# Routed rows of a top-2 expert layer: scattered once into a table sorted by turn and fetched by plain loads, in place of an indirect gather per turn

## The reference, cut to what matters

```python
g_prob = softmax(t @ w_grp + b_grp);  g_idx = top_k(g_logits, 1)          # 1 of 4 groups
e_in_group = (t @ w_exp + b_exp)[group of the token]
top_v, top_i = top_k(e_in_group, 2);  top_w = softmax(top_v) * g_w        # 2 of 4 experts
a = einsum('td,edf->tef', t, w_gate_e);  u = einsum('td,edf->tef', t, w_up_e)
hid = silu(a) * u * combine[..., None]
return einsum('tef,efd->td', hid, w_down_e)                                # D_EXPERT = 512
```

## Time and profile before

| | |
|---|---|
| time, median of 3 executions | 1935.51 us (1934.56 to 1939.46) |
| span of the profiled execution | 1934.0 us |
| PE / DVE / ACT / POOL busy | 91% / 28% / 11% / 8% of the span |
| DMA over the span | 531.09 MB, 275 GB/s |
| software (POOL) queue | 97.15 MB, 14.1% of 16 engines |
| chain that ended last, PE / issue / DMA / DVE | 65% / 12% / 10% / 5% |

### The profile page before, as it was taken

How to read it: one execution, slowest core, us unless ns; L and a number is a source line. 1 busy time by engine, 2 the same in 40 slices (tenths; PEclk the granted TensorE clock), 3 DMA queues, 4 the chain that set the end, 5 groups by cost and what they waited for, 6 DMA issues and landing times.

```text
span 1934.0 us, 27785 instructions
## 1 busy us (share of the span) xinstructions
PE 1767.3 (91%) x11144; PEld 1114.0 (58%) x11144; DVE 534.1 (28%) x1152; ACT 210.8 (11%) x405; POOL 156.1 (8%) x274
## 2 busy tenths in 40 slices
PE   7799999999998999978889999997699998998998
PEld 4366666666666877756667777775333333333335
DVE  3100000000047744455553111003323222231233
ACT  2010000000001201102222100002110001000002
POOL 1011111111110001410000000000100000000000
PEclk9899999999999999988899999998799899999999
DMA  9997887677516335538999874242499999999992
GB/s 371 402 380 273 317 297 285 246 262 289 198 49 201 100 111 168 207 119 298 385 392 368 325 271 134 88 174 94 146 368 406 397 397 384 410 404 383 401 391 96
DMA packets 154570, 531.09 MB, mean 275 GB/s; under 512 B 17701, under 2 KB 61899, under 8 KB 131803
## 3 DMA queue, kind: packets, MB, share of 16 engines
q1 hardware_dynamic: 128834, 432.24, 58.9%
q0 software_dynamic: 17088, 97.15, 14.1%
q10 hardware_dynamic: 8578, 0.73, 0.4%
HBM read 510.94 MB, written 19.15 MB: 274 GB/s over the span
## 4 chain that ended last, share of the span: by engine, by line
PE 65%; issue 12%; DMA 10%; DVE 5%; SPq 4%; DVEq 1%; POOL 1%; ACT 1%; POOLq 1%; ACTq 0%; PEldq 0%
PE ps L652 62%; DMA ring<-in_w_up_e_dram 4%; DMA ring<-in_w_ada_dram 2%; PE ps L662 2%; SPq L399 2%; DMA xT<-in_w_ada_dram 2%; SPq L393 2%; DMA xT<-in_w_in_dram 2%; POOL work L537 1%; DVE z L1468 1%; DVE z L1459 1%; DVEq L2115 1%; DVE ring L1465 1%; POOLq L536 0%; DVE ring L1837 0%
## 5 line engine op out<-in xcount | busy, mean ns | idle before, releaser
L652 PE MATMUL ps<-hT,ring 128*128 128x288 f32 x2304 | 585.3, 410 | 5.3 <-PE ps L652 3.6
L652 PEld LDWEIGHTS ps<-hT,ring 128*128 128x128 f32 x2304 | 430.0, 190 | 169.7 <-issue 59.1
L652 PE MATMUL ps<-ring,work 128*64 128x512 f32 (+1 forms) x1280 | 273.4, 617 | 25.3 <-DMA ring<-in_w_ada_dram 12.2
L652 PE MATMUL ps<-z,ring 128*128 128x288 f32 (+1 forms) x1040 | 255.5, 407 | 4.5 <-PE ps L652 2.7
L1468 DVE COPY z<-ps 128x256 f32<-128x256 f32 (+7 forms) x98 | 64.3, 660 | 677.1 <-PE ps L652 656.9
L652 PE MATMUL ps<-ring,z 32*32 32x256 f32 (+3 forms) x3744 | 213.9, 396 | 21.2 <-DVE z L1468 11.2
L652 PEld LDWEIGHTS ps<-z,ring 128*128 128x128 f32 x1040 | 196.4, 190 | 62.8 <-issue 7.5
L652 PEld LDWEIGHTS ps<-ring,work 128*64 128x64 f32 (+1 forms) x1280 | 77.8, 134 | 181.4 <-issue 165.7
L652 PEld LDWEIGHTS ps<-ring,z 32*32 32x32 f32 (+3 forms) x3744 | 108.5, 114 | 115.2 <-issue 108.3
L1263 ACT ACTIVATE z<-ps 128x512 f32<-128x512 f32 (+4 forms) x108 | 60.1, 602 | 860.3 <-PE ps L652 850.4
L1465 DVE SCALAR_TENSOR_TENSOR xT<-ps,modT,xT 128x256 f32<-128x256 f32 x160 | 70.8, 480 | 254.3 <-PE ps L652 254.2
(11 more groups left out here) (209 smaller groups left out, 877.4 us busy)
## 6 DMA issues: line engine op xcount, KB each, us to landing
ring<-in_w_in_dram SPq DMA_DIRECT2D x36, 2048.0 KB, 14.3
ring<-in_w_gate_e_dram SPq DMA_DIRECT2D x32, 2048.0 KB, 12.7
ring<-in_w_up_e_dram SPq DMA_DIRECT2D x32, 2048.0 KB, 18.4
ring<-in_w_down_e_dram SPq DMA_DIRECT2D x32, 2048.0 KB, 15.0
ring<-in_w_ada_dram SPq DMA_DIRECT2D x16, 2048.0 KB, 20.5
z<-in_w_ada_dram POOLq DMA_DIRECT2D x32, 1024.0 KB, 7.9
xT<-in_w_ada_dram POOLq DMA_DIRECT2D x32, 1024.0 KB, 6.7
ring<-in_cache_v_dram SPq DMA_DIRECT2D x64, 512.0 KB, 5.8
```

Source lines behind the costliest of these rows:

```text
L652: return nc.tensor.matmul(o, lhsT, rhs, start=start, stop=stop, skip_group_check=free)
```

## The change

The table `h_rows` goes; in its place stands `h_sorted`, with NWIN * W = 1664 rows of 8 KB, row `at_turn * 64 + at_slot`. At `ob_ready`, behind the load of `x_kept`, POOL zeroes 4 KB in each partition of `work2` and writes it over the whole table with 13 DMAs of 1 MB. DVE computes the six columns of destinations (`places`) and signals `places_ready` before the rest of the list; POOL then issues six indirect DMAs, each scattering 96 rows of `hTok` (each token twice). DVE waits for the clears before it writes `listing`, and for the scatters before it clears `y_two`. SP fetches the 64 rows of turn 0 after the scatters, those of turn 1 after `hs_turned` 1, and in the loop those of turn w + 2 between the fourth and the fifth weight load of turn w + 1. POOL's loop is gone.

```diff
@@ SP
+            def sorted_rows(turn):
+                sp.dma_start(hg, h_sorted[ds(turn * W, W), :]).then_inc(sem("hg_full"), 16)
-            def expert(e, turn):
+            def expert(e, turn, rows_of=None):
                 for n in range(6):
                     s = (MOE + n) % SLOTS
+                    if n == 4 and rows_of is not None:
+                        sp.wait_ge(sem("hs_turned"), rows_of)
+                        sorted_rows(rows_of)
                     sp.wait_ge(sem(f"ring_free{s}"), turn + freed(MOE + n))
...
             expert(0, 0)
+            sp.wait_ge(sem("rows_sorted"), 16 * 2 * NT)
+            sorted_rows(0)
+            sp.wait_ge(sem("hs_turned"), 1)
+            sorted_rows(1)
             sp.wait_ge(*step("table_ready"))
...
-                expert(e, w + 1)
+                expert(e, w + 1, w + 2)
@@ POOL
             pool.dma_start(xflat, x_kept).then_inc(sem("x_back"), 16)
+            pool.memset(cleared, 0.0)
+            pool.drain()
+            for n in range(NWIN * W // P):
+                pool.dma_start(h_sorted[n * P:(n + 1) * P, :].rearrange("p (a n) -> p a n", a=2),
+                               cleared.unsqueeze(1).to_broadcast([P, 2, 1024])).then_inc(sem("rows_cleared"), 16)
...
-            for c in range(NT):
-                pool.wait_ge(sem("htok_copied"), 4 * c + 4)
-                pool.dma_start(h_rows[c * TT:(c + 1) * TT, :], hTok[:, c, :]).then_inc(sem("h_stored"), 16)
-            def gather(w):
-                pool.tensor_copy(take, token_i[:, ds(w, 1)])
-                pool.drain()
-                pool.indirect_dma_start(hg, None, h_rows, bass.IndirectOffsetOnAxis(ap=take, axis=0)).then_inc(sem("hg_full"), 16)
-            pool.wait_ge(sem("h_stored"), 16 * NT)
-            pool.wait_ge(*step("list_ready"))
-            gather(0)
-            pool.wait_ge(sem("hs_turned"), 1)
-            gather(1)
+            pool.wait_ge(*step("places_ready"))
+            pool.wait_ge(sem("htok_copied"), 4 * NT)
+            pool.wait_ge(sem("rows_cleared"), 16 * (NWIN * W // P))
+            for i in range(2 * NT):
+                pool.indirect_dma_start(h_sorted, bass.IndirectOffsetOnAxis(ap=places[:, i:i + 1], axis=0),
+                                        hTok[:, i // 2, :], None).then_inc(sem("rows_sorted"), 16)
...
-            with pool.Fori(0, last_turn) as it:
-                pool.wait_ge(sem("hs_turned"), it + 2)
-                gather(it + 2)
@@ DVE
             pick(at_slot, within)
+            pick(at_turn, turn)
+            stt(places, at_turn, float(W), at_slot, ALU.mult, ALU.add)
+            v.drain()
+            v.sem_inc(reach("places_ready"), 1)
             tt(in_slot, ...)
-            pick(at_turn, turn)
...
+            v.wait_ge(sem("rows_cleared"), 16 * (NWIN * W // P))
             for n in range(2):
                 tt(listing[:, :, :, n], ...)
...
-            copy(token_i, sums[0:W, :, 0])
             copy(listed, sums)
-            v.drain()
-            v.sem_inc(reach("list_ready"), 1)
             nc.vector.memset(spots, 0.0)
-            v.wait_ge(sem("h_stored"), 16 * NT)
+            v.wait_ge(sem("rows_sorted"), 16 * 2 * NT)
             nc.vector.memset(y_two, 0.0)
```

More of the change, by code:

```diff
@@ L63 @@
         "gla_sample_ready os_turned_copied ms_a_ready rs_a_ready rs_a_inverted "
-        "kv_tok_ready gla_scratch_free f_ready s_new_copied ob_ready work_free ms2_ready logits_copied member_ready pos_ready "
-        "table_ready list_ready").split(),
+        "kv_tok_ready gla_scratch_free f_ready s_new_copied ob_ready work_free ms2_ready logits_copied member_ready places_ready pos_ready "
+        "table_ready").split(),
 }
@@ L125, in build @@
         eps_col = vcol[:, 150:151]
-        h_rows = nc.dram_tensor("h_rows", [T, D], F32).ap()
+        h_sorted = nc.dram_tensor("h_sorted", [NWIN * W, D], F32).ap()
         x_kept = nc.dram_tensor("x_kept", [P, KT * T], F32).ap()
@@ L248, in build @@
         now = ms[:, 2 * NWIN:2 * NWIN + 2]
-        token_i = rstd[0:W, 0:NWIN].bitcast(I32)
-        take = rstd[0:W, 64:65].bitcast(I32)
+        places = rstd[0:TT, 0:2 * NT].bitcast(I32)
+        cleared = work2[:, 0:1024]
         spots = z[:, 3 * D:3 * D + T]
@@ L639, in _ @@
                                vcol[:, V_GF:V_GF + KT].unsqueeze(2).to_broadcast([P, KT, P]), ALU.mult).then_inc(sem("gf_spread"), 1)
-            last_turn = pool.value_load(wtab[0:1, 1:2], min_val=NE - 1, max_val=NWIN - 3)
-            with pool.Fori(0, last_turn) as it:
-                pool.wait_ge(sem("hs_turned"), it + 2)
-                gather(it + 2)
             pool.wait_ge(sem("gla_prompt_stored"), 16)
```

## The result

| | before | after |
|---|---|---|
| median | 1935.65 us (1934.56 to 1939.46, 4 runs) | 1967.89 us (1961.33 to 1972.5, 4 runs) |
| span of the profiled execution | 1934.0 us | 1959.8 us |
| router's logits product to the first product of turn 0 | 40.3 us | 52.7 us |
| first product of turn 0 to the end of the span | 556.5 us | 568.5 us |

The changed kernel is slower: ratio 1.0159, 95% interval 1.0133 to 1.0185, 32.2 us on the medians. That is under 2%, but clear of the noise. The prediction was no change, 1935.0 us, with a range up to 1949.

A forecast was written before the change was run, and what follows sets the result against it. The prediction took DMA to bound the turns, with PE close behind. The loop's -10.5 us and the start's +10 us gave -0.5 us, all other terms 0: 1935.0 us on the median, no change, range 1925 to 1949.

The forecast's parts named there:

- What bounds the kernel: In the turns: DMA engines fully busy at 395 GB/s, slowed behind each gather, with PE close behind.
- PE's cap: In the turns: 18 us is all PE can give back, from weight waits and the lower clock after them.
- The loop, -10.5 us: Plain loads replacing 15 gathers lose 1.7 us each instead of 2.4, saving 0.7 us a turn.
- The place in the queue, 0: In the loop: the fetch standing behind the gate and up loads on SP's queue costs nothing.
- The cover: In the loop: 32 PE products, 7.8 us, hide the fetch; without them it costs up to 2.5 us a turn.
- Rival 1: In the loop: the destination causes the dip, so the loop gives 0 and the start costs 10 us: 1945.5 us; chance 0.27.
- The rule on the ports: For fetches onto partitions 0 to 63: only 8 of 16 DMA ports are reached, so transfers run at half rate.
- Rival 2: In the loop: only the gather is slow, plain rows cost their bytes, PE becomes the bound: 1927.5 us; chance 0.18.
- Rival 3: Before the turns: scatters slower than stores (start +15) or clears reaching PE: 1942 us, 1950 with rival 1; chance 0.10.
- The start, +10 us: Before the first turn: six serial scatters, then SP's load, delay the first product by 10 us, ends 5.5 and 15.
- The clears, 0: Writing 13.6 MB during the PE-bound up projections hides in idle DMA capacity; at most a few us otherwise.
- The clear of `y_two`, 0: Before the first turn, behind the scatters: its 2 us hide under the fetch and the transposes, 8 us.

The follow-up runs named there:

- r3_actq: Changed kernel, with ACT issuing the loop's plain fetches on its own DMA queue instead of SP: 1945.55 us, ratio 1.0065.
- r9_poolq: Changed kernel, with POOL issuing every fetch of sorted rows as a plain DMA on its software queue: 1946.7 us, ratio 1.0051.
- r2_wide: Changed kernel, with each loop fetch writing the same 512 KB onto 128 partitions of 4 KB (rows partly wrong): 1932.2 us, ratio 0.9987.
- r5_shift: Changed kernel, with each loop fetch writing its 64 rows onto partitions 32 to 95 instead of 0 to 63 (wrong rows): 1933.61 us, ratio 0.9992.
- r8_pair_gather: Kernel before, with one indirect gather of 128 rows onto 128 partitions for every two turns, full computation: 1922.0 us, ratio 0.994.
- r7_clears: Kernel before, with only the 13 clears added, to a table nobody reads, and DVE waiting for them before the list: 1934.63 us, ratio 0.9999.
- r6_half_bytes: Changed kernel, with each loop fetch cut to 4 KB of each of the 64 rows, same partitions (wrong rows): 1932.1 us, ratio 0.999.

## Why the prediction was wrong, point by point

- **What bounds the kernel: right.** The turns are bound by DMA, the loss sits in the dips, and PE stands close behind. PE's cap was put at 18 us; the kernels without dips have a rest of 540 to 544 us where before has 556.6, so it is 12 to 17 us.
- **The loop, -10.5 us: the first step that failed.** It took the plain fetch to lose 1.7 us instead of the gather's 2.4, from the one plain narrow load in the trace of before, scaled by bytes. Measured in the turns, the plain fetch's dip loses 2.3 to 2.4 us from a second queue, the gather's 2.5, and the rests are 556.2 and 557.3 us against 556.6: the saving is 0. The load of 32 rows was a poor sample. It ran in another stage among other loads, and a dip of 2 us between stretches that are themselves unsteady gives a loss with little precision.
- **The place in the queue, 0: the second and larger one.** It cost +18.4 us (rest 575.0 against 556.6). The cover held, PE never waits for the rows. But the step looked only at who waits for the fetch. That the fetch in the weights' own queue would slow the weights more than it did in a second queue wasn't asked. r3_actq and r9_poolq against after show it.
- Together the two steps make 10.5 + 18.4 = 28.9 us of the miss of 32.9. The ends that were put on a fetch's loss, 0 to 2.4 us, held no value above the gather's, although nothing in the trace ruled one out. The range therefore had no room for a loop that gets worse.
- **Rival 1, that the dip belongs to the destination: right in its mechanism** (r2_wide, r5_shift, r8_pair_gather), and r3_actq and r9_poolq are that rival as it was priced, 1945.5 us against 1945.55 and 1946.7. That the first agrees to 0.1 us is luck: its start cost 12.3 us and not 10, and its router began 2.1 us earlier. Its evidence was in rows 10 and in the lone gather of rows 8; it was given 0.27 where the forecast had 0.45. The change as built adds the queue's 18 us to it. The rule on the ports that spoke against the change (the Trainium skill, "SBUF — State Buffer", section "Door 1: The DMA port swizzle") thus held in direction. The estimate of a 1.2 us loss from its 218 GB/s is under all that was measured in the turns for a whole fetch onto these partitions, 2.3 to 3.1 us in the dip.
- **Rival 2, that only the gather is slow: wrong.** A plain load dips as deep or deeper. **Rival 3, slower scatters or clears that reach PE: wrong** as priced: the start stayed under its +15 us and the clears cost nothing.
- **The start, +10 us: right**, 12.4. The terms: from the places to the last row in the table 18.5 us predicted, from the first issue 19.7 measured; fetch 4.8 and 4.74. The first issue took 1.63 us and each further one 0.91 to 0.93, 0.30 us apart, where 0.98 was assumed. The data of the six scatters took some 17 us where 15.9 were put: 320 GB/s at first, over the store's 297 that was taken, and then a tail at a DMA share of 0.60.

```profile
1365.00:1383.00 18.00, 2.80 (x12) 2.63 (x12) 3.18 (x14) 0.00 (x0) 8.27 (x7) 0.50 0.82 262
1367.00:1378.00 11.00, 1.86 (x9) 1.69 (x8) 1.52 (x8) 0.00 (x0) 6.88 (x5) 0.50 0.98 320
1378.00:1382.00 4.00, 0.00 (x0) 0.00 (x0) 0.00 (x0) 0.00 (x0) 0.00 (x0) 0.50 0.60 193
```

- **The clears, 0: right** (r7_clears, 1934.63). **The clear of `y_two`, 0: right**, 1.76 us, under the fetch:

```profile
1383.62 1.76 DVE L2087 MEMSET z<- 128x2048 f32 x1 [14.21 <-DMA h_sorted<-z,rstd]
```

So on the median: start 12.4, destination 0 (the gather paid it too), the weights' queue 18.4, together 30.8 of 32.2 us. The other 1.4 us lie ahead of the router in the profiled execution and are about what executions differ by.

**Open:** why a narrow fetch costs more time in the queue of the weights than in a second one, with dips that in after are no deeper; whether its place in that queue matters; and why two half fetches in it cost less than one whole.

## What to carry to other kernels

Where a stage is bound by DMA, look at which partitions a small transfer lands on before asking how it is issued. Here a gather turned into a plain load gained nothing, and as many bytes on 128 partitions, or on 32 to 95, gained all that the next bound allowed. The fastest of the complete versions was the old gather, for two turns at once onto 128 partitions: 1922.0 us, 0.6% under before, clear of the noise. Keep a transfer onto partitions 0 to 63 out of the queue that carries the weights (18 us here); and count what a preparation costs in series where the stage behind it can't catch up, as the 12 us of this scatter.

When the trace has only one sample of the thing to be priced, from another stage, take its ends wide on both sides of what it replaces, worse as well as better.

## What the runs showed of the hardware

- 512 KB onto partitions 0 to 63 took 2.3 to 2.5 us from concurrent weight loads beyond their own bytes when they came from a second queue (ACT's, POOL's, indirect or plain), and in the weights' own queue 2.4 us in one kernel and 3.1 in another, while the time of both grew by 18 us more. 256 KB onto them took 1.4 us (r6_half_bytes). Onto partitions 32 to 95, or onto all 128, no loss was visible in the time (410 and 413 GB/s, PE then being the bound).
- In such a dip the DMA engines count as fully busy (1.00 to 1.03) at 231 to 293 GB/s. The busy share alone doesn't show it.
- Issues of an indirect scatter of 96 rows took 0.91 us of POOL each and the first one 1.63 us, with 0.30 us between them; a gather of 128 rows took 1.07. Six such scatters, 4.72 MB, moved 320 GB/s in their first 11 us.
